# The sample stage of a hybrid decoder step, computed in four column groups of 32 rows

## What is computed

```python
def sparse_attend(q, kg, vg, ok):
    s = jnp.einsum('btgrd,btkgd->btgrk', qg, kg) * A_HEAD_DIM ** -0.5
    s = jnp.where(ok[:, :, None, None, :], s, NEG_INF)
    p = jax.nn.softmax(s, axis=-1)
    return jnp.einsum('btgrk,btkgd->btgrd', p, vg)
# retention of one chunk (4 rows of a sample sequence)
att = jnp.einsum('bnhid,bnhjd->bnhij', q, k) * dmask
intra = jnp.einsum('bnhij,bnhje->bnhie', att, v)
cross = jnp.einsum('bnhid,hi,bnhde->bnhie', q, q_dec, r_prev)
state = chunk_dec * state + jnp.einsum('bnhjd,hj,bnhje->bnhde', k, k_dec, v)
```

## Time and profile before

| quantity | value |
|---|---|
| median of three timed executions | 3819.58 us (3815.45 to 3823.34) |
| the profiled execution | 3819.86 us, span 3818.3 us |
| mean granted TensorE clock | 0.929 |
| busy: PE, DVE, ACT, POOL | 3297.2 (86%), 1881.2 (49%), 1376.7 (36%), 862.4 us (23%) |
| sample stage | 1801.9 to 1978.5, 176.6 us |
| PE busy in it | 119.8 us |

### The profile page before, as it was taken

One profiled execution on the slowest core, in us unless ns is written; L12 is line 12 of the kernel. 1 busy time (PEld: TensorE's weight loads), 2 busy tenths in 40 slices (PEclk: granted clock), 3 DMA queues, 4 the chain that ended last, 5 costly groups with the idle time before them and its releaser, 6 DMA issues. The chain is left out here.

```text
span 3818.3 us, 47913 instructions
## 1 busy us (share of the span) xinstructions
PE 3297.2 (86%) x15513; PEld 1821.7 (48%) x15513; DVE 1881.2 (49%) x3899; ACT 1376.7 (36%) x2827; POOL 862.4 (23%) x1714
## 2 busy tenths in 40 slices
PE   7997889888888888676769999999999738988998
PEld 4553434444444444343534444444455436656665
DVE  0000575677777878742301341523414556665764
ACT  2211126556656576663112111121121134433442
POOL 3331333221212111000000000000000037773772
PEclk9998999999999999788889999999999859997999
DMA  5556666544433332001524111011110132224221
GB/s 182 176 170 215 203 208 204 180 146 139 132 111 117 105 111 70 14 4 53 189 96 184 38 57 66 27 62 50 56 50 23 44 124 86 93 100 122 77 79 61
DMA packets 256377, 403.06 MB, mean 106 GB/s; under 512 B 46900, under 2 KB 132093, under 8 KB 253981
## 3 DMA queue, kind: packets, MB, share of 16 engines
q1 hardware_dynamic: 233632, 383.56, 30.9%
q0 software_dynamic: 4096, 8.40, 0.9%
q10 hardware_dynamic: 18432, 8.40, 0.8%
HBM read 318.39 MB, written 103.15 MB: 110 GB/s over the span
## 5 line engine op out<-in xcount | busy, mean ns | idle before, releaser
L706 PE MATMUL PB<-wb,hT_ahead 128*128 128x512 f32 x832 | 429.0, 643 | 42.2 <-DMA wb<-in_w_in_ab 38.1
L2119 PE MATMUL QB<-hT,w_c 128*128 128x512 f32 x1024 | 449.4, 593 | 0.0
L717 PE MATMUL PT<-ident,sm 128*128 128x128 f32 x1088 | 193.5, 302 | 130.7 <-ACT sm L856 128.4
L2119 PEld LDWEIGHTS QB<-hT,w_c 128*128 128x128 f32 x1024 | 190.3, 190 | 216.9 <-issue 216.9
L302 PE MATMUL P0A<-w_all,hT 128*128 128x512 f32 (+1 forms) x816 | 266.9, 487 | 0.0
L717 PEld LDWEIGHTS PT<-ident,sm 128*128 128x128 f32 x1088 | 132.4, 152 | 264.9 <-ACT sm L856 155.2
L866 ACT COPY ptT<-PT 128x512 f32<-128x512 f32 (+3 forms) x320 | 164.2, 518 | 247.5 <-PE PT L717 246.8
L2819 PE MATMUL RPJ<-w_co,oT 128*128 128x512 f32 x544 | 249.0, 607 | 4.4 <-ACT oT L3003 3.4
L2088 PE MATMUL QA<-w_c,hT 128*128 128x512 f32 (+1 forms) x768 | 249.7, 481 | 3.4 <-DVE crow L2388 2.3
L706 PEld LDWEIGHTS PB<-wb,hT_ahead 128*128 128x128 f32 x832 | 153.2, 204 | 205.1 <-issue 165.3
L2062 PE MATMUL QS<-w_o,yT 128*128 128x512 f32 x544 | 239.4, 599 | 0.7 <-ACT yT L2249 0.7
(11 more groups left out here) (436 smaller groups left out, 5385.6 us busy)
## 6 DMA issues: line engine op xcount, KB each, us to landing
wb<-in_w_in_ab SPq DMA_DIRECT2D x272, 512.0 KB, 3.9
out_c_all<-crow SPq DMA_DIRECT2D x256, 64.0 KB, 1.6
out_pr_all<-pr_out SPq DMA_DIRECT2D x17, 546.0 KB, 3.6
pra<-out_pr_all SPq DMA_DIRECT2D x16, 546.0 KB, 4.7
x_rows<-in_x_all SPq DMA_DIRECT2D x17, 512.0 KB, 5.8
out_hT_all<-hT SPq DMA_DIRECT2D x17, 512.0 KB, 2.9
yab<-out_yab_all SPq DMA_DIRECT2D x17, 512.0 KB, 5.1
xin<-in_x_all SPq DMA_DIRECT2D x17, 512.0 KB, 4.5
```

Of the source, the lines that this page charges most:

```text
L706: ins = pe.matmul(b_bank(g, n)[:, :], h_of(g)[:, 2 * q + k, :], wb[:, u % 4, k, :], start=(q == 0 and k == 0), stop=(q == 3 and k == 1))
L717: ins = pe.transpose(PT[v % 2][:, k * P:(k + 1) * P], sm[:, 2 * (r % 2) + a, c * CH + k * P:c * CH + (k + 1) * P], ident[:, :])
L2119: ins = pe.matmul(PB[b % 2][:, 0:N], w_c[:, c, b * P:(b + 1) * P], hT[:, c, 0:N], start=(c == 0), stop=(c == KD - 1))
```

## The change

Scores, values and retention output of the sample rows are computed in four column groups of TensorE. The rows of a key head are now ordered (pair i, head r, half a, row t), so that pair i owns the 32 rows 32i to 32i+31; batches 2i and 2i+1 form pair i. A score matmul has a stationary operand of 32 columns and writes 32 rows of PSUM; so do the value matmuls, with 128 moving columns in place of 512, and the retention output, one head a group. The mask is stored four times, by pair, in device memory in the new row order (16 stores of 8 rows at places 60 to 90 in place of one at -5), loaded as 128 rows, and added by DVE in the same instruction that takes the maximum and writes `sc`. ACT alone evacuates the keys. The gates `za` and `zb` are loaded by twelve DMAs of their own in the layout of the results, between the key pairs 0 and 1 on SP, and ACT's first instructions, ahead of the key copies, wait for them. The retention chain comes before key pair 1, pairs 2 and 3 after it, and the group norm works on 128 rows of 128. Transposes of weights run one unit ahead, and ACT and DVE copy them in turn. The result is stored straight from that layout.

```diff
-            i, a = b % HB, b // HB
+            i, a = divmod(b, 2)
...
-    add(-5, "sp", "s_store")
+    for i in range(HB):
+        add(60 + 10 * i, "sp", "s_store", i)
...
-            def s_store():
+            def s_store(i):
                 sp.wait_ge(S["s_mask_ready"], after(1))
-                sp.dma_start(io["mb_s"][:, :], s_row).then_inc(S["s_mask_stored"], 16)
+                for r in range(4):
+                    sp.dma_start(io["mb_s"][SR * i + 2 * DT * r:SR * i + 2 * DT * (r + 1), :],
+                                 isc[2 * DT * i:2 * DT * (i + 1), 1, :]).then_inc(S["s_mask_stored"], 16)
...
+            keys_in(0)
             sp.wait_ge(S["zeroed4"], after(2))
             for h in range(RH):
                 lo = HD * (h % 2)
                 sp.dma_start(rs[lo:lo + HD, :, h, :], io["state_ret"][:, h].rearrange("b d e -> d b e"))\
                   .then_inc(S["rs_loaded"], 16)
+            for dst, src in ((rmask[:, :, :, :], io["rmask_s"][0:SR, :].rearrange("p (a c q) -> p a c q", a=2, c=2)[:, :, :, 0:SR]),
...
+                             (mb[:, :], io["mb_s"])):
+                sp.dma_start(dst, src, allow_slow_non_contiguous=True).then_inc(S["c4_loaded"], 16)
+            for h in range(RH):
+                sp.dma_start(gng[h * SR:(h + 1) * SR, :], io["gn_ret"][:, h * RV:(h + 1) * RV].partition_broadcast(SR),
+                             allow_slow_non_contiguous=True).then_inc(S["c4_loaded"], 16)
+            for h in range(RH):
+                sp.dma_start(zb[h * SR:(h + 1) * SR, :], io["pr_all"][NEW, C_ZB + h * RV:C_ZB + (h + 1) * RV])\
+                  .then_inc(S["z4_loaded"], 16)
+            for i in range(HB):
+                for g in range(2):
+                    cols = slice(C_ZA + 4 * g * HD, C_ZA + 4 * (g + 1) * HD)
+                    sp.dma_start(za[i * SR:(i + 1) * SR, g, :],
+                                 io["pr_all"][SEQ + 2 * DT * i:SEQ + 2 * DT * (i + 1), cols].rearrange("q (r d) -> r q d", d=HD))\
+                      .then_inc(S["z4_loaded"], 16)
+            keys_in(1)
...
+            sp.wait_ge(S["rs_stored"], after(64))
+            values_in(0)
             sp.wait_ge(S["kt_ps"], after(8 * HB))
+            values_in(1)
...
+            for b in range(DB):
+                for h in range(RH):
+                    ins = pe.matmul(PA[1][h * SR:(h + 1) * SR, 0:RV], qbm[:, h // 2, b, :], rs[:, b, h, :], start=False,
+                                    stop=(b == DB - 1))
             ins.then_inc(S["ro4_ps"], 1)
             pe.wait_ge(S["kd4"], after(1))
             ret_add(0)
             ret_add(1)
-            keys(2)
+            keys(1)
             ret_add(2)
             ret_add(3)
+            keys(2)
             keys(3)
...
                     for i in range(HB):
-                        pe.matmul(PS[u % 2][:, 0:w], qm[:, g, i, :], K_T[g][:, i, c0:c0 + w], start=(i == 0),
-                                  stop=False)
-                    pe.matmul(PS[u % 2][:, 0:w], rep4[:, :], mb128[:, c0:c0 + w], start=False, stop=True)\
-                      .then_inc(S["s4_ps"], 1)
+                        ins = pe.matmul(PS[u % 2][i * SR:(i + 1) * SR, 0:w], qm[:, g, i, :], K_T[g][:, i, c0:c0 + w],
+                                        start=True, stop=True)
+                    ins.then_inc(S["s4_ps"], 1)
...
+                        for i in range(HB):
+                            ins = pe.matmul(PO[g][i * SR:(i + 1) * SR, 0:P], ptT[:, u % 2, k * P + i * SR:k * P + (i + 1) * SR],
+                                            V[:, pg % 8, 2 * i:2 * i + 2, g * HD:(g + 1) * HD], start=(pg == 0), stop=False)
...
+            turn_p(0)
+            for u in range(10):
+                if u < 9:
+                    turn_p(u + 1)
+                times_v(u)
...
         @block.scalar
         def _(act):
+            act.wait_ge(S["z4_loaded"], after(16 * (RH + 2 * HB)))
+            act.activation(gb[:, :], zb[:, :], ACT.Tanh, scale=0.5)
...
+                    dve.tensor_tensor_reduce(sc[g][:, c0:c0 + w], PS[u % 2][:, 0:w], mb[:, c0:c0 + w], 1.0, -3e38, ALU.add,
+                                             ALU.max, mx8[:, u:u + 1]).then_inc(S["s4_mx"], 1)
```

## The result

The changed kernel takes 3757.4 us (median of four, 3751.2 to 3761.3) against 3819.5 us, ratio 0.984 (95% interval 0.982 to 0.985): 62.1 us less, where 74.7 were forecast. Beside twenty-one executions of the kernel before on another chip it gave the same ratio again, 0.984. Its profiled execution took 3757.5 us, span 3755.9. The forecast, 3745, is 12.4 us too low; the range 3731 to 3764 holds the result.

What follows compares the result with a forecast made beforehand. In the sample stage PE was taken to set scores and values, evacuation the head. Savings of 12.6 + 26.8 + 1.1 + 26.0 + 5.7 = 72.2, and 2.5, give 74.7 us off 3819.9: 3745, range 3731 to 3764.

Steps and rivals of the forecast that it cites:

- output and change of stage: End of the sample stage: three DVE steps and four stores, 10.4 us for 16.1, 5.7 less.
- stages ahead of the sample stage: Prompt stage with the mask's stores moved: -2.5 us, bounds -5 and +2.
- Head: Sample stage up to the first score product: it comes at 1865 instead of 1877.6, 12.6 us less.
- merely changes its cause: Head: PE's stall stays, as ACT's first key copy waits for gate loads until about 1827; the DVE copy stood at 1828.7.
- Scores: Score products of the sample stage: four column groups run at once, 1.1 us a chunk, 10.5 us in all, 26.8 less.
- the bank's turn: Scores: PE passes, DVE's add-and-maximum and semaphores on one PSUM bank take some 2.1 us for two chunks.
- Values: Value products: 1.65 us a unit, about 1 us of wait for part B, 16.5 us for 42.5, 26.0 less.
- the worse case: Values: each of 18 tile-shape changes costs 0.27 us in place of 0.17, making the sum 2 us worse.
- Rivals 1, 2 and 3: Sample stage: two column groups at once, 3759 us (chance 0.17); none, 3791 (0.06); gate loads 5.86 us each, 3853 (0.03).
- Rival 4: Head or prompt stage at bad bounds (ACT at 1832, +2 at mask stores, longer part-B wait): 3755, chance 0.12.
- the price of the sixteen stores: Prompt stage: sixteen issues at 0.45 us instead of one, and more bytes among the loads, cost 0 to 4 us.
- the other term: Prompt stage: without PE's 11.28 us wait for `wb`, `ret_out` moves from 543.1 to about 538, 4.5 us gained.

Runs made afterwards that it cites:

- e_tanh: The changed kernel with ACT's wait for the gates and its two tanh moved behind its first 8 key copies: 3746.8 us, ratio 0.981.
- a_again: The changed kernel once more, unedited, beside the kernel before on the same chip: 3760.0 us, ratio 0.984.
- s_g2: The changed kernel with its score products on two column groups instead of four, same work on other numbers: 3761.2 us.
- s_g1: The changed kernel with its score products all on one column group, same work on other numbers: 3776.6 us.
- b_move1: The kernel before with its one mask store moved from place -5 to 60: 3820.3 us against 3823.2, ratio 0.9996.
- c_move16: The kernel before with its mask store made into 16 stores of 8 rows at places 60 to 90: 3828.7 us, ratio 1.0018.

## Why the prediction came out as it did

| step | forecast | measured |
|---|---|---|
| stage start to first score product | 63.1 | 62.9 |
| first key copy on ACT, after the start | 25.1 | 25.6 |
| scores | 10.5 | 9.2 |
| pause to the first value product | 3.9 | 3.1 |
| values, the wait for part B in it | 16.5, 1 | 19.0, 3.7 |
| output and change of stage | 10.4 | 9.4 |
| stages ahead of the sample stage | -2.5 | +5.1 |
| last stage | 0 | +5.8 |

- **Head: right, every step within 2 us of its forecast place.** The gate loads, one engine's evacuation and the retention output in one run came as described. (The idle times of 7.93 and 6.67 us that it reads as PE's are those of the weight loads; PE's own were 7.69 and 6.43. Nothing hangs on it.) That the stall "merely changes its cause" was e_tanh's point: had it been costed as a removable wait, a better change could have been named before the run.
- **Scores: right on the disputed point.** Four groups at once, where the only row showed two. The chunk was 0.95 us for 1.1: the bank's turn of 2.1 us for two chunks was 1.89.
- **Values: unit right (1.60 for 1.65), wait too small.** Part B landed 82.2 us into the stage, forecast 82.1. That agreement has some luck in it: part A was issued 0.8 us early, and B landed 0.9 us later behind it than forecast. Head, scores, pause and the first two units were 0.2, 1.3, 0.8 and 0.7 us shorter than forecast, and these 3.0 us went wholly into the wait (0.6 by the forecast's own times). What the work ahead gained was no gain, since the landing didn't move with it. The units behind the wait, two of them at half clock, took 12.0 for 11.5. In a_again, the same kernel, the two units ahead of the wait ran at a lower clock (4.8 us for 3.3), and the wait was 1.98. The changes of tile shape between products and transposes cost 0.17 and 0.20 us of idle time, not the 0.27 of the worse case.
- **Rivals 1, 2 and 3** are out: s_g2 and s_g1 show what two groups and one would have looked like, and the 23 loads between state and second key pair took 15.9 us in all, 0.69 each, the dearest 2.66 (`rmask`), not 4.2. For two groups the rival asked 14 us in all, 5.3 of them in the scores; s_g2, which has two groups in the scores alone, lost 6.4 there, and its stage was 1.2 us longer. (The rival's own terms add up to 3758, not 3759.)
- **Rival 4 came nearest.** The result lies outside the forecast's own band of 3736 to 3753 and 2 us from the 3755 of rival 4. Two of that rival's three conditions came true, the prompt stage past its bad bound and a longer wait for part B; the third did not: ACT started 25.1 us into the stage, where the bad bound was 30.1 (its 1832.18 is read in a stage that itself began 5 us later).
- **The step that failed is the price of the sixteen stores.** "0 to 4 us", 2 taken; it measured 6.6 us in the row block that holds them (8.5 between the medians of b_move1 and c_move16). The prediction priced an issue at 0.45 us from a row with quiet queues; between the weight loads one took 0.81 (12.9 us for 16), and in a row 0.91 (14.5). And it took the `wb` loads to be late only by their own landing, while three groups of them stood behind stores. The condition was written down ("if PE waits on `wb` between 560 and 580, the mask's stores cost what they had saved"); PE did, at 578. And it had no term for what such a wait does to the clock, which is 3.0 of the 6.6 us. With the other term, a gain of 4.5, nothing was wrong in idle time (4.3 in b_move1). The 7.6 us by which the sample stage began too late are then 4.6 from this term and 4.1 from the two row blocks after it, which vary from run to run, less 1.1 elsewhere.
- **The last stage's 5.8 us** are no step of the prediction: equal code took 762.1 to 774.8 us. They and the start of the sample stage (1801.8 to 1809.1 with the same sixteen stores ahead of it) bound what a forecast made against one profile of each kernel can say: some 10 us either way, an estimate from these spreads. Single executions of the changed kernel reach past the range's end of 3764 (3765.4 and 3766.8 us in a_again, whose median is 3760.0).

## What to carry to other kernels

Price a DMA issue where it is going to stand: one store of 32 rows took 0.46 us alone, and stores of 8 rows took 0.8 to 0.9 each among other loads or in a row. The cost is paid by the load queued behind them, and by the clock after the wait for that load. Ask of every wait at the head of an engine's program who else needs that engine first; moving two activations behind eight copies was worth 10 us in the profiles. When two profiles of nearly the same kernel differ, split the difference into busy and idle time of the engine that bounds it, and follow one instruction that recurs through both, before you explain it: it shows at which places they part.

## What the runs showed of the chip that was not expected

- Column groups overlapped completely: 3.43, 1.72 and 0.86 us for eight passes of 512 columns on one, two and four groups, with no cost of issue to be seen.
- A wait of PE of 3.3 to 4.3 us was followed by a loss of nearly as much in the clock (3.0 us on average): the row block around it took 55.4 to 57.3 us at a granted clock of 0.94 to 0.97, against 50.1 us at 1.00 without it.
- Issues of one queue slow down with what another issues: 3.2 to 3.9 us for the four state loads alone, 11.74 beside sixteen small loads from ScalarE.
- The last stage, equal code in all kernels, took from 762.1 to 774.8 us, with PE busy for 618 to 635 us at granted clocks of 0.88 to 0.86.
